# Hybrid decoder layer on one core: 160 gathered rows beside 352 dense columns, split rotary scores, and the attention norm applied after the output projection

## What is computed

```python
o_attn = rmsnorm(mla(...), g_out_attn)          # 8 heads, query = 128 plain + 64 rotary columns
o_sgu  = rmsnorm(chunked_sgu(...), g_out_sgu)
h = h + concatenate([o_attn, o_sgu]) @ w_out    # 2048 x 2048
h = h + peer(rmsnorm(h, g_ffn), ...)
# peer, per token and head (8 heads): the 16 best of 128 x 128 experts, gates = softmax
#   hidden = gelu(u_exp[expert] . a);  out += gate * hidden * v_exp[expert]
gate = sigmoid(rmsnorm(h, g_ple) @ w_gate);  h = h + gate * (p @ w_proj)
```

## Time and profile before

| | |
|---|---|
| runs | 3066.82, 3071.43, 3072.93 us; median 3071.43 |
| profiled execution | 3070.68 us, of which the span of the trace is 3068.9 us |
| PE / PEld busy | 3039.3 us (99%) / 2854.3 us (93%) |
| DVE / ACT / POOL busy | 2225.5 us (73%) / 1061.5 us (35%) / 1212.6 us (40%) |
| moved by DMA | 768.59 MB, mean 250 GB/s |
| granted TensorE clock, mean | 0.996 |

### The profile page before, as it was taken

One profiled execution on the slowest core, in us unless ns is written; L12 is line 12 of the kernel. 1 busy time (PEld: TensorE's weight loads), 2 busy tenths in 40 slices (PEclk: granted clock), 3 DMA queues, 4 the chain that ended last, 5 costly groups with the idle time before them and its releaser, 6 DMA issues.

```text
span 3068.9 us, 42590 instructions
## 1 busy us (share of the span) xinstructions
PE 3039.3 (99%) x16888; PEld 2854.3 (93%) x16888; DVE 2225.5 (73%) x2944; ACT 1061.5 (35%) x1328; POOL 1212.6 (40%) x702
## 2 busy tenths in 40 slices
PE   9999999999999999999999999999999999999998
PEld 7888668899999999999999999999999999999887
DVE  5565653478778767777777668888888888996545
ACT  5234442323333333333333343333333333334422
POOL 1010000018888788788887122332232333340000
PEclk9999999999999999999999999999999999999999
DMA  8472212235445499999989789889989898984222
GB/s 301 164 245 90 96 56 95 83 125 135 125 123 138 125 371 346 335 353 345 359 315 369 282 318 378 350 349 362 356 356 364 354 362 355 354 329 163 96 96 96
DMA packets 191487, 768.59 MB, mean 250 GB/s; under 512 B 68608, under 2 KB 121872, under 8 KB 129392
## 3 DMA queue, kind: packets, MB, share of 16 engines
q1 hardware_dynamic: 90768, 407.45, 36.2%
q0 software_dynamic: 81632, 335.12, 30.5%
q10 hardware_dynamic: 18944, 24.14, 2.3%
HBM read 714.00 MB, written 52.62 MB: 250 GB/s over the span
## 4 chain that ended last, share of the span: by engine, by line
PE 95%; DVE 2%; issue 1%; ACT 1%; DMA 1%; SPq 0%; DVEq 0%; ACTq 0%
PE ps L1669 31%; PE ps L1671 31%; PE ps L1670 31%; PE ps L1846 1%; ACT wH L590 1%; DMA raw<-s_v 1%; PE ps L1865 1%; DVE ssum L1000 1%; PE ps L1845 1%; PE ps L1908 0%; DVE wL L988 0%; PE ps L1855 0%; DVE hT L1638 0%; PE ps L1847 0%; DVE smax L1225 0%
## 5 line engine op out<-in xcount | busy, mean ns | idle before, releaser
L1669 PE MATMUL ps<-aH,wH 128*128 128x368 f32 (+2 forms) x3088 | 1075.2, 348 | 3.0 <-DVE aL L1245 2.1
L1670 PE MATMUL ps<-aL,wH 128*128 128x368 f32 (+2 forms) x3088 | 1071.7, 347 | 0.0
L1671 PE MATMUL ps<-aH,wL 128*128 128x368 f32 (+2 forms) x3088 | 1071.6, 347 | 0.0
L590 ACT ACTIVATE wH<-raw 128x2048 fp32r<-128x2048 f32 x333 | 637.5, 1915 | 990.7 <-PE ps L1671 854.2
L988 DVE TENSOR_TENSOR wL<-raw,wH 128x2048 fp32r<-128x2048 f32 x333 | 783.9, 2354 | 190.0 <-ACT wH L590 189.1
L526 POOL DMA_INDIRECT gates<-gates_r,idx_d x384 | 746.1, 1943 | 370.1 <-DVE gates_r L1389 237.6
L1669 PE MATMUL ps<-actH,wH 128*128 128x368 f32 x2048 | 673.8, 329 | 0.0
L1671 PE MATMUL ps<-actH,wL 128*128 128x368 f32 x2048 | 673.5, 329 | 0.0
L1670 PE MATMUL ps<-actL,wH 128*128 128x368 f32 x2048 | 673.4, 329 | 0.0
L1669 PEld LDWEIGHTS ps<-aH,wH 128*128 128x128 f32 x3088 | 580.0, 188 | 42.3 <-issue 3.2
L1670 PEld LDWEIGHTS ps<-aL,wH 128*128 128x128 f32 x3088 | 580.1, 188 | 38.7 <-issue 1.0
(11 more groups left out here) (260 smaller groups left out, 1960.4 us busy)
## 6 DMA issues: line engine op xcount, KB each, us to landing
raw<-s_pu SPq DMA_DIRECT2D x128, 1024.0 KB
raw<-s_pv SPq DMA_DIRECT2D x128, 1024.0 KB
gates<-zeros POOLq DMA_DIRECT2D x23, 1024.0 KB, 8.4
pre<-ut ACTq DMA_DIRECT2D x128, 184.0 KB
pre_in<-pre SPq DMA_DIRECT2D x128, 184.0 KB
gate_in<-gates SPq DMA_DIRECT2D x128, 184.0 KB
raw<-s_out SPq DMA_DIRECT2D x16, 1024.0 KB
raw<-s_pq SPq DMA_DIRECT2D x16, 1024.0 KB
```

Source lines behind the costliest of these rows:

```text
L590: A(wH[parity][:, :], raw[at_n][:, :], ACT.Copy).then_inc(hi_ready, 1)
L1669: mm(out, wh, xh, start=start, stop=False)
L1670: mm(out, wh, xl, start=False, stop=False)
L1671: return mm(out, wl, xh, start=False, stop=stop)
```

## The change

1. `BT` goes from 16 to 32: `TD` is 352 columns, 160 tokens are gathered. `SETS` becomes 4 and `B_PICKS` 32, so there are 160 picks, 96 of them beside v-slots 2 to 119. `dots_b` and `pick_wb` now lie in `dots` and `pick_w`.
2. In u-slots with picks and in v-slots only an add may stand ahead of `lo`; a dot always follows it.
3. The rotary part of the scores is split: `ropeQ` holds for each head the high half in its own 64 partitions and the low half in the other 64, `ropeKH` and `ropeKL` the key's halves; two fp32r products replace the fp32 one. PE waits for `rope_lo` of a head at its first item.
4. The attention half is no longer normalised ahead of the projection. Each head's output is multiplied by its gain and split during attention (`attn_head` on ACT, `attn_low` on DVE). Its eight tiles of the projection are summed in a PSUM bank of their own, and `residual` multiplies that bank by the norm's factor, adds the other bank and adds to `hT`: three DVE operations for one.
5. The sgu half is scaled inside attention (items 9 to 16), its high halves follow at items 18 to 25, four low halves at 22 to 25. The projection starts with sgu tiles 4 to 7. Three of the four reloads of x wait for the last score.

```diff
-BT = 16
+BT = 32
-PARTS = SETS // HEADS
-B_PICKS = TOPK // PARTS
+B_PICKS = A_PICKS // SETS
...
+                    if (s, m) == (0, 3):
+                        act.wait_ge(rope_ready, 1)
+                        act.wait_ge(sgu_ready, 8)
+                        A(ropeKH[:, :], krT[:, :], ACT.Copy).then_inc(rope_hi, 1)
+                    if s == 1:
+                        r = head_rows(m)
+                        act.wait_ge(rope_ready, 2 + m // 2)
+                        A(ropeQ[r, m, :], qT[r, 8 + m // 2, :], ACT.Copy).then_inc(rope_hi, 1)
...
+            def attn_head(h):
+                act.wait_ge(o_copied, h + 1)
+                square("attn", h, mixT[:, h, :])
+                A(aH[:, h, :], mixT[:, h, :], ACT.Copy, scale=gain("attn", h)).then_inc(attn_hi, 1)
...
+            def rope_low(h):
+                dve.wait_ge(rope_hi, 2 + h)
+                r, other = head_rows(h), head_rows(h + 1)
+                V.tensor_tensor(ropeQ[other, h, :], qT[r, 8 + h // 2, :], ropeQ[r, h, :].bitcast(F), ALU.subtract).then_inc(rope_lo, 1)
...
+                if 5 <= n + 4 < HEADS:
+                    rope_low(n + 4)
+                if 22 <= n < 26:
+                    sgu_lo(n - 22)
+                if 0 <= n - 9 < SGU_TILES:
...
-                V.tensor_tensor(hT[:, 2 * i + j, :], hT[:, 2 * i + j, :], ps[:, j, :], ALU.add).then_inc(h_mixed, 1)
+                V.tensor_tensor(tmp[j][:, :], ps[:, 2 + j, :], rstdB[:, :], ALU.mult).then_inc(mix_scaled, 1)
+                dve.wait_ge(mix_scaled, 2 * i + j + 1)
+                V.tensor_tensor(tmp[j][:, :], tmp[j][:, :], ps[:, j, :], ALU.add).then_inc(mix_summed, 1)
+                dve.wait_ge(mix_summed, 2 * i + j + 1)
+                V.tensor_tensor(hT[:, 2 * i + j, :], hT[:, 2 * i + j, :], tmp[j][:, :], ALU.add).then_inc(h_mixed, 1)
...
                     steps = range(v_step(g, q), v_step(g, q + 1))
-                    for o in steps[0:1]:
+                    early = [o for o in steps[0:1] if o % 2 == 1]
+                    for o in early:
                         pick_step(o)
                     v_low(g, q)
-                    for o in steps[1:]:
+                    for o in steps[len(early):]:
                         pick_step(o)
...
-                    mm(o, qT[r, 8 + h // 2, t], krT[r, 0:w], start=False, stop=False)
+                    if qt == 0:
+                        pe.wait_ge(rope_lo, 2 + h)
+                    mm(o, ropeQ[:, h, t], ropeKH[:, 0:w], start=False, stop=False)
+                    mm(o, ropeQ[r, h, t], ropeKL[r, 0:w], start=False, stop=False)
...
-                ins = three(ps[:, j, :], wH[j][:, w], wL[j][:, w], aH[:, k, :], aL[:, k, :], i == 0, i == KD - 1)
+                ins = three(ps[:, j if k >= 8 else 2 + j, :], wH[j][:, w], wL[j][:, w], aH[:, k, :], aL[:, k, :], i % 8 == 0, i % 8 == 7)
```

More of the change, by code:

```diff
@@ L349, in trunk_layer @@
         _at = 0
-        for name, k in (("mix", 16), ("cq", 4), ("ckv", 2), ("sgu", 8), ("attn", 8), ("ffn", 16), ("ple", 16)):
+        for name, k in (("mix", 16), ("cq", 4), ("ckv", 2), ("sgu", 8), ("ffn", 16), ("ple", 16)):
             N_SC[name] = _at
@@ L506, in _ @@
             pool.wait_ge(act_lo, N_SC["sgu"])
-            for i in range(4):
+            for i in (3, 0, 1, 2):
+                if i == 0:
+                    pool.wait_ge(score_done, HEADS * NT)
                 pool.dma_start(hT[:, 4 * i:4 * i + 4, :], a["x"][:, 4 * i:4 * i + 4, :]).then_inc(x_again, 16)
             pool.wait_ge(act_lo, N_SC["ffn"])
+            pool.wait_ge(attn_lo, HEADS)
             pool.dma_start(keys[:, :, :, :], a["keys"]).then_inc(keys_loaded, 16)
@@ L1513, in _ @@
                 steps = range(u_step(c), u_step(c + 1))
-                late_dot = c >= KEYS - GROUP and len(steps) == 1 and steps[0] % 2 == 0
-                for o in steps[0:0 if late_dot else 1]:
+                early = [o for o in steps[0:1] if o % 2 == 1]
+                late = [o for o in steps[0:1] if o % 2 == 0 and c >= KEYS - GROUP]
+                for o in early:
                     pick_step(o)
                 lo(nu + c + 1, (c + 1) % 2)
-                for o in steps[1:]:
+                for o in steps[len(early) + len(late):]:
                     pick_step(o)
@@ L1521, in _ @@
                     weight_lo(c - KEYS + GROUP, c - KEYS + GROUP, 0, pre_in[c % 2])
-                if late_dot:
-                    pick_step(steps[0])
+                for o in late:
+                    pick_step(o)
             def v_begin(g, q, m, i):
@@ L1889, in _ @@
                     pe.wait_ge(h_mixed, 2 * i + j - 1)
-                    tile(S0["out"] + 2 * i + j, j, j)
+                    out_tile(S0["out"] + 2 * i + j, j)
             pe.wait_ge(h_mixed, 13)
-            tile(S0["out"] + 14, 0, 0)
+            out_tile(S0["out"] + 14, 0)
             pe.wait_ge(h_mixed, 14)
-            tile(S0["out"] + 15, 1, 1, after=lambda ins, j: ins.then_inc(a_read, 1))
+            out_tile(S0["out"] + 15, 1, last=True)
             def scores(h, b, s):
```

125 lines of the change are left out of this document (66 added, 59 removed).

## The result

The changed kernel takes 3101.4 us (median of 3095.3 to 3105.8) against 3070.0 for the kernel before (3066.8 to 3072.9): ratio 1.0099, 95% interval 1.0087 to 1.011. It is **31 us slower**, where 37 us faster was forecast. The profiled execution is one of 3098.8 us, with a span of 3097.1. PE is busy for 54 us less than before (3039.3 to 2985.0), and still the end comes 28 us later: the saved columns turned into idle time.

The account below looks back on a forecast made before the run. PE was taken to set the pace from 615 on, with DVE becoming slowest in v-slots. From 3070.7 us, -44.2 + 17.7 - 6.5 - 4 = -37 us gave 3034, stated as 3033 us, range 2985 to 3082.

Parts of the forecast that it names:

- Fewer columns: All slots: 352 columns take 160.0 ns a matmul, a slot 7.68 us, saving 81.9 us if PE keeps the pace.
- I take the 44.2 in full: The 138 slots other than v-slots with picks: PE's whole saving of 44.2 us was counted.
- a fifth of their time free: U-slots: DVE and POOL, busy 75% and 80%, were taken to have room for the faster pace.
- the rule alone changes the sum by nothing: V-slots: exclusion of two-SBUF-input VectorE instructions and SBUF-reading GpSimd ones was given no cost, also for the 32 b-picks.
- V-slots: 118 v-slots with picks: DVE asks for 8.18 us, taken as 8.15 a slot, 17.7 us more than before.
- One buffer's round: V-slots: a row buffer's round, from issue to end of add, takes 18.7 of 18.9 us available.
- rival B: V-slots: gathers slow to 15.5 us, row buffers set an 8.8 us slot, 3110 us; chance 0.13 (over 3065).
- Attention: Attention stage: the split rotary product saves 11 us, less waits and added operations, net -6.5 us.
- Start of the projection: Output projection: the 2.08 us wait and the half-clock stretch go, the second tile pair waits 2.3 us; net -4 us.
- A: V-slots: PE keeps the pace and DVE's lateness is absorbed, 7.75 us a slot, 2987 us; chance 0.22 (under 3004).
- C: Attention: PE's clock falls to 0.50 for half of it, 40 us more, 3073 us; chance 0.05 with other cases.
- or PE waiting in u-slots as well: U-slots: listed among the signs that would show the forecast wrong; u-slots were forecast at 7.68 us.

Follow-up runs that it names:

- e5: The changed kernel without every fourth scatter-add of the gates, so three stand between two gathers (part of the work left out): 3073.9 us.
- e13: The changed kernel with gathers of half a row and adds of the v stage over 1024 of 2048 elements (work left out): 3016.0 us.
- e2: The changed kernel with the old order of steps: a slot's first step, dot or add, ahead of the low half again: 3073.7 us.
- e7: The changed kernel with gathers of half a row, 8 KB in place of 16 (half the sum is wrong): 3070.8 us.
- e9: The changed kernel with the adds of the v stage cut to 1024 of 2048 elements (work left out): 3047.1 us.
- e4: The changed kernel with BT back at 16 and the old order of steps, which leaves attention and projection: 3065.9 us.
- all four corners: The changed kernel (3101.4 us), with the old width (3068.0), with the old order of steps (3073.7), and with both undone (3065.9).
- e8: The changed kernel with 72 picks in place of 64 beside u-slots, three scatter-adds between gathers, the last 19 at the end: 3053.4 us.
- e12: The changed kernel with 72 picks beside u-slots and 220 scatter-adds spread evenly to end with gather 66, dots late everywhere: 3056.9 us.

## Why the prediction was wrong, point by point

**Fewer columns: right as a price.** 7.68 us a slot is what e5 shows in u-slots and e13, with 7.69, in v-slots, and the last 20 slots of the changed kernel before 1238 us took 7.73.

**"I take the 44.2 in full": the step that failed.** It tested DVE and the transfers of the u-slots against the new pace and passed over POOL with "a fifth of their time free". A POOL at 80% was full: with 0.3 us of issuing in front of each of its five instructions a pick and the waits for its own scatter-adds, it had 8.6 us of waits for DVE in 440 left. Its line reads, before, in the window 1240 to 1680:

```profile
POOL rows L545 <- DVE hT L1487: 8.6, 6, 3.0
```

That is 2% of air, where 352 columns take 4%. e5 gives the price, 34 us of u-slots between four scatter-adds and three. The busy share of an engine whose instructions each need an issue doesn't say how much it can still take; the time that it waits for others does.

**The later dots in u-slots: not in the sum at all.** I costed the order only in v-slots and gave it a gain there. In u-slots it makes POOL's scatter-adds start nearer to the beginning of adds: 28 us between e2 and the changed kernel, at an unchanged number of instructions. The section of the skill that I weighed was the right one, and I applied it to DVE's dots only, with the result that "the rule alone changes the sum by nothing". It also holds for those dots: `rows<-rows,b_tok`, with both inputs in SBUF, takes 2.62 us in the mean in the v stage after, and the dots with one in PSUM 2.28:

```profile
L1506 DVE SCALAR_TENSOR_TENSOR rows<-rows,ps 128x2048 f32<-128x2048 f32 x62 | 141.4, 2281 | 23.6 <-DMA rows<-uv_rows,idx_s 23.6
...
L1506 DVE SCALAR_TENSOR_TENSOR rows<-rows,b_tok 128x2048 f32<-128x2048 f32 x31 | 81.3, 2622 | 9.8 <-DMA rows<-uv_rows,idx_b 9.8
```

The mean is made of two kinds: the 14 b-dots that start while POOL's `tensor_tensor` is running take 3.04 us, the other 17 take 2.28; the 34 dots with an input in PSUM that start beside it take 2.28 too. The three b-dots of my window were too few to show it.

**V-slots: the mechanism right, the size short by 0.20 us a slot.** By the waits above, over the 115 slots of the window:

| term, us a slot | forecast | after |
|---|---|---|
| DVE busy | 7.51 | 859.25 / 115 = 7.47 |
| wait for the weight, dot and add in a row | 0.19 | 21.5 / 115 = 0.19 |
| wait for `actH` | 0.25 | 31.4 / 115 = 0.27 |
| waits for rows | 0.23 | 33.4 / 115 = 0.29 |
| wait for `wH` | none | 12.1 / 115 = 0.11 |
| sum | 8.18, taken as 8.15 | 8.33 |

Each named term came out near its size. The one that was missing is the wait for `wH`: with two buffers DVE can't make the next low half before PE has left the slot before, so a DVE that is early for once must stop, and what it gains can't be kept for the next late row. (Busy time and waits add up to the slot in any case; that it is these that lengthen it rests on e7, e9 and e13.) The half clock behind PE's waits comes on top where it holds the next `wH` back; how much of the 8.35 is due to it no run isolates.

**One buffer's round.** 18.7 us was forecast. The dots of 66 to 127 follow each other at 10.2 us, a round of 20.4, but as the consequence of slower slots: from a gather's issue to its landing it takes 11.0 us in the mean over all picks, as before (11.2). The transfers at 372 GB/s did not lengthen it, and rival B's mechanism fell, though its time of 3110 is the nearest of the four.

**Attention: right sign, too large.** From the first to the last score product the time fell from 76.6 to 71.6 us, 5.1 where 6.5 was forecast. The split product costs more than I put: of 1.4 us a head saved on it, 0.6 arrived in the distance from head to head. Added up start to start over the stage, the plain and the rotary products of the scores took 44.0 us before and 36.0 after, so 1.0 a head was saved on PE; and its waits for `prob` and `probT` grew from 2.0 to 5.2 us, which is the other 0.4.

**Start of the projection.** The wait of 2.08 us and the stretch at clock 0.50 are gone, as forecast. The next one late is the one that was named; timeline of PE after, the second pair of tiles, for which 2.3 us were forecast:

```profile
442.11 0.51 PE L1699 MATMUL ps<-aH,wH 128*128 128x512 f32 x1 [2.36 <-DVE wL L1002]
```

Attention and projection together are worth 5.5 us in e4, half of 10.5. In the changed kernel's trace they are worth 7.3: 5.1 in attention and 2.2 from the last score product to `wH` copy 50. The start of attention alone varies by 4 us between the traces (336.7 to 341.0), so the one number is no firmer than the other.

**The rivals.** A (2987) needed a DVE with air. C put the clock's loss into attention, where it stayed at 1.00; in the slots it is 21 us, which no case had. The case that happened, POOL full in u-slots and slower by the order, stands among none of them: "or PE waiting in u-slots as well" is named last as a sign of being wrong, without a price.

## What to carry to other kernels

When the bounding engine is made faster, every other queue must be held against the new pace, and for one that issues DMAs the air is the time that it waits for others in the stage, not one minus its busy share: POOL at 80% busy had 2% left. Two edits may each cost next to nothing in a stage and 28 us together, when one takes the air that the other needs, so an experiment that undoes one at a time finds them both guilty; only all four corners told. And where two lanes have nearly the same demand, lightening one of them gives a fraction of what its sum promises (0.34 us of 0.87 in e9), and moving work to another stage can give more (0.48 us a slot in e8 for eight picks).

## What the hardware showed that was not expected

- A scatter-add that POOL starts while DVE runs an instruction with both inputs in SBUF ends 1.3 to 1.45 us after the end of that instruction (308 of the 314 cases in the u-slots of before, after, e2 and e12); without one it takes 1.50 to 1.53 us in the mean, and never over 1.6 in the changed kernel. So the phase of the two engines is worth up to 2 us an instruction. It works one way only: DVE's instructions that start while a scatter-add is running are as long as without it (2.29 us for 51 `wL`), and only those that start beside POOL's `tensor_tensor` are held (3.04 us for 14 dots in place of 2.28).
- PE's pace behind ten of its 48 waits, of 2.1 to 4.8 us, fell to 0.29 us a product of 352 columns from 0.16 (the clock's lower level), and 28% of the idle time was lost once more in that way (21 us behind 75).
- The two lanes of the v-slots met at 372 GB/s, with the transfers' share at 0.94: more than the 358 GB/s that the page "HBM Reference" of the Trainium skill (Specifications) gives for one core, as the earlier trace rows already showed; the page says itself that a core alone measures more.
